# Forget bias and causal mask of a two-layer attention trunk: from bias matmuls and a mask addition to one fused vector operation with the bias read back from DRAM

## The reference

```python
f_logit = (proj[..., 4 * WIDTH:] + b_f_bias[j]).astype(jnp.float32)
log_f = jax.nn.log_sigmoid(f_logit).transpose(0, 2, 1)
...
c = jnp.cumsum(log_f, axis=-1)
...
sc = (jnp.einsum('bhqd,bhkd->bhqk', qb, k, preferred_element_type=jnp.float32) * scale
      + (cq[..., :, None] - c[..., None, :]))
sc = jnp.where(kpos[None, :] <= tq[:, None], sc, -jnp.inf)
p = jax.nn.softmax(sc, axis=-1)
```

## Time and profile before

| | us |
|---|---|
| median of 3 runs | 577.65 (577.51 to 578.0) |
| profiled execution, its time | 577.4 |
| its span | 575.6 |
| TensorE busy | 559.3 |
| VectorE / ScalarE / GpSimd busy | 346.8 / 249.4 / 266.7 |

### The profile page before, as it was taken

How to read it: one execution, slowest core, us unless ns; L and a number is a source line. 1 busy time by engine, 2 the same in 40 slices (tenths; PEclk the granted TensorE clock), 3 DMA queues, 4 the chain that set the end, 5 groups by cost and what they waited for, 6 DMA issues and landing times.

```text
span 575.6 us, 9794 instructions
## 1 busy us (share of the span) xinstructions
PE 559.3 (97%) x3131; PEld 518.3 (90%) x3131; DVE 346.8 (60%) x825; ACT 249.4 (43%) x760; POOL 266.7 (46%) x318
## 2 busy tenths in 40 slices
PE   5699999999999999999999999999999999999998
PEld 4589999999999999988888999999999999998887
DVE  4935859585867677674462674747474747473621
ACT  5534535444453535432454653535353544442400
POOL 5555636354545545333646472727272726260700
PEclk9989999999999999999999999999999999999999
DMA  9532404141313222213432242515140526040221
GB/s 286 164 91 64 139 19 129 29 119 40 106 53 92 65 81 73 73 37 107 110 88 73 75 108 39 108 40 118 28 120 25 116 30 136 16 131 9 73 92 55
DMA packets 77066, 48.34 MB, mean 84 GB/s; under 512 B 3952, under 2 KB 71280, under 8 KB 77040
## 3 DMA queue, kind: packets, MB, share of 16 engines
q1 hardware_dynamic: 77040, 48.02, 30.8%
HBM read 45.91 MB, written 2.10 MB: 83 GB/s over the span
## 4 chain that ended last, share of the span: by engine, by line
PE 94%; DVE 2%; SPq 1%; DMA 1%; ACT 1%; issue 0%; POOL 0%
PE banks L298 25%; PE banks L299 25%; PE banks L300 25%; PE banks L405 5%; PE banks L390 3%; PE banks L357 2%; PE banks L375 2%; PE banks L379 2%; PE banks L374 2%; DMA first_raw<-in_a_w_in_dram 1%; PE banks L378 1%; PE banks L318 1%; SPq L233 1%; DVE sin_t L701 1%; SPq L250 0%; DVE hT_lo L681 0%
## 5 line engine op out<-in xcount | busy, mean ns | idle before, releaser
L964 POOL TENSOR_TENSOR w_lo<-w_raw,w_hi 128x512 fp32r<-128x512 f32 x152 | 193.6, 1300 | 69.9 <-ACT w_hi L517 69.9
L298 PE MATMUL banks<-w_hi,hT_hi 128*128 128x384 f32 x512 | 176.4, 344 | 8.2 <-DVE qkn L736 6.4
L300 PE MATMUL banks<-w_hi,hT_lo 128*128 128x384 f32 x512 | 172.2, 336 | 0.0
L299 PE MATMUL banks<-w_lo,hT_hi 128*128 128x384 f32 x512 | 172.2, 336 | 0.0
L298 PEld LDWEIGHTS banks<-w_hi,hT_hi 128*128 128x128 f32 x512 | 96.8, 189 | 10.0 <-DVE qkn L736 7.0
L979 POOL TENSOR_TENSOR msq<-ssq,eps 128x2 f32<-128x2 f32 x64 | 13.7, 215 | 188.2 <-ACT junk L544 188.2
L517 ACT ACTIVATE w_hi<-w_raw 128x512 fp32r<-128x512 f32 x152 | 87.5, 646 | 24.6 <-DMA w_raw<-in_b_w_in_dram 14.4
L299 PEld LDWEIGHTS banks<-w_lo,hT_hi 128*128 128x128 f32 x512 | 96.9, 189 | 0.1
L300 PEld LDWEIGHTS banks<-w_hi,hT_lo 128*128 128x128 f32 x512 | 96.7, 189 | 0.0
L544 ACT ACTIVATE junk<-banks 128x128 bf16<-128x128 f32 x128 | 34.1, 273 | 117.2 <-PE banks L300 117.2
L814 DVE RECIPROCAL gz<-gz 128x128 f32<-128x128 f32 x64 | 58.1, 930 | 0.5
(11 more groups left out here) (104 smaller groups left out, 877.5 us busy)
## 6 DMA issues: line engine op xcount, KB each, us to landing
w_raw<-in_b_w_in_dram SPq DMA_DIRECT2D x64, 256.0 KB, 3.6
w_raw<-in_a_w_in_dram SPq DMA_DIRECT2D x56, 256.0 KB, 2.9
w_raw<-in_w_out_dram SPq DMA_DIRECT2D x32, 256.0 KB, 3.0
xs<-in_x_dram SPq DMA_DIRECT2D x4, 512.0 KB, 6.6
first_raw<-in_a_w_in_dram SPq DMA_DIRECT2D x8, 256.0 KB, 5.8
out_dram<-xs SPq DMA_DIRECT2D x7, 256.0 KB, 2.5
gz<-in_norm_g_dram SPq DMA_DIRECT2D x2, 512.0 KB, 4.2
cos_t<-in_rope_cos_dram SPq DMA_DIRECT2D x1, 256.0 KB, 5.6
```

The lines of the kernel that those rows point to most:

```text
L298: pe.matmul(dst, ah, bh, start=first and m == 0, stop=False)
L299: pe.matmul(dst, ah, bl, start=False, stop=False)
L300: mm = pe.matmul(dst, al, bh, start=False, stop=last and m == n - 1)
L964: pool.tensor_tensor(w_lo[:, slot, k, :], raw, f32(w_hi[:, slot, k, :]), ALU.subtract).then_inc(wlo_set, by)
```

## The change

The four bias matmuls per head, `crows`, `pick`, `onehot` and the separate mask additions go. Instead:

- VectorE's `maxima` makes one fused operation per tile: it adds a row operand in SBUF to the scores in the bank, multiplies by −1, writes the result to `probs` in SBUF and keeps its minimum, which is the negated row maximum. In layer 0 the operand is `strip` (zeros, and the mask in its last 128 columns), in layer 1 `bias_of[t]`. A one-element memset of `gate` stands ahead of three of the four and takes the wait for the scores.
- ScalarE's `exps` reads `probs` (not the banks), with scale −1, and writes it in place; it waits for each tile's maximum by itself.
- After the scan SP writes c (8 x 512) to a DRAM tensor `c_rows` and, when that has landed, reads the head's row back spread over 128 partitions, once per tile at the tile's width (four transfers, 640 KB, per head). They go where layer 0's rotary tables were. For head 0 this stands ahead of head 2's weight chunks; for head h (1 to 7) it stands after chunk 4 of the job h+1, and waits for the maxima of head h−1, since there is one buffer.
- GpSimd adds the mask to the diagonal block of each of the four (`mask_bias`): for head 0 at the end of `first`, for head h+1 in period h after chunk 4 and before `rstd_qk` of tile 2.
- `f_all` moves to the buffer `rot`, `f_exp` to `sin_t`.

```diff
@@ sync: load_job, load_bias
-            def load_job(layer, h, src_of):
+            def load_job(layer, h, src_of, bias=False):
...
                     load_chunk(w_raw[:, k % RAW, :], src_of(k), raw_in[k % RAW])
+                    if bias and k == RAW:
+                        load_bias(h - 1)
...
+            def load_bias(h):
+
+                wait(sp, max_set, TILES * (HEADS + h) if not isinstance(h, int) or h else 0)
+                for t in T_ORDER:
+                    row = c_rows[bass.ds(h, 1), 0:P * (t + 1)].rearrange("o n -> (o n)")
+                    sp.dma_start(bias_of[t], row.partition_broadcast(P)).then_inc(bias_in, 16)
+
             for layer in range(LAYERS):
-                with sp.Fori(0 if layer else 2, HEADS) as h:
-                    load_job(layer, h, head_src(layer, h))
+                if layer == 1:
+                    for h in range(2):
+                        load_job(layer, h, head_src(layer, h))
+                    sp.wait_ge(f_step, 4)
+                    sp.dma_start(c_rows, f_all).then_inc(c_stored, 16)
+                    sp.wait_ge(c_stored, 16)
+                    load_bias(0)
+                with sp.Fori(2, HEADS) as h:
+                    load_job(layer, h, head_src(layer, h), bias=layer == 1)
                 for c in range(OUT_CHUNKS):
-                    load_job(layer, HEADS + c, out_src(layer, c))
+                    load_job(layer, HEADS + c, out_src(layer, c), bias=layer == 1 and c == 0)
@@ tensor: scores
-                if layer == 1:
-                    pe.wait_ge(c_set, 1)
-                    pe.wait_ge(pick_set, h + 1)
...
-                    if layer == 1:
-
-                        pe.matmul(dst, pick[:, s, :], crows[:, 0:w], start=False, stop=False)
@@ scalar: exps
-                wait(act, p_turned, 3 * g)
...
-                    act.wait_ge(max_set, TILES * g + (n + 1 if n < 2 else TILES))
-                    act.activation(probs[:, P_COL[t]:P_COL[t] + w], banks[:, bank, col:col + w], ACT.Exp,
-                                   bias=negmax[:, t:t + 1], accum_out=rowsum[:, t:t + 1]).then_inc(exp_set, 1)
+                    part = probs[:, P_COL[t]:P_COL[t] + P * (t + 1)]
+                    act.wait_ge(max_set, TILES * g + n + 1)
+                    act.activation(part, part, ACT.Exp, bias=negmax[:, t:t + 1], scale=-1.0,
+                                   accum_out=rowsum[:, t:t + 1]).then_inc(exp_set, 1)
@@ vector: maxima
-                wait(dve, exp_set, TILES * g)
-                mask_tile(0)
+                wait(dve, exp_set, TILES * g)
+                wait(dve, p_turned, 3 * g)
+                if layer == 1:
+                    dve.wait_ge(bias_set, h + 1)
                 for n, t in enumerate(T_ORDER):
                     bank, col = S_AT[t]
-                    if n + 1 < TILES:
-                        mask_tile(n + 1)
-                    dve.wait_ge(mask_added, TILES * g + n + 1)
-                    dve.tensor_reduce(negmax[:, t:t + 1], banks[:, bank, col:col + P * (t + 1)], AX.X, ALU.max,
-                                      negate=True).then_inc(max_set, 1)
+                    w = P * (t + 1)
+                    if n < 3:
+                        dve.wait_ge(s_done, 3 * g + n + 1)
+                        dve.memset(gate[0:1, n:n + 1], 0.0)
+                    dve.tensor_tensor_reduce(out=probs[:, P_COL[t]:P_COL[t] + w], in0=banks[:, bank, col:col + w],
+                                             in1=bias_of[t] if layer else strip[:, SEQ - w:], scale=-1.0,
+                                             scalar=NO_MIN, op0=ALU.add, op1=ALU.min,
+                                             accum_out=negmax[:, t:t + 1]).then_inc(max_set, 1)
@@ gpsimd: mask_bias, at the end of first (layer 1) and in period
+                if layer == 1:
+                    mask_bias(0)
+
+            def mask_bias(h):
+
+                pool.wait_ge(bias_in, 16 * TILES * (h + 1))
+                for t in T_ORDER:
+                    diag = bias_of[t][:, P * t:P * (t + 1)]
+                    added = pool.tensor_tensor(diag, diag, strip[:, SEQ - P:], ALU.add)
+                added.then_inc(bias_set, 1)
...
                 split_w(layer, h + 2, s, (4,))
+                if layer == 1:
+                    mask_bias(h + 1)
                 rstd_qk(layer, h + 1, 2)
```

More of the change, by code:

```diff
@@ L27 @@
 MASKED = -3.0e38
+NO_MIN = 3.0e38
 LO_ROW = 32
@@ L83, in build_trunk @@
         sin_t = sb("sin_t", [P, TILES, 2, P])
-        crows = sb("crows", [P, SEQ], F32R)
-        pick = sb("pick", [P, 2, P], F32R)
         ident = sb("ident", [P, P])
-        mask = sb("mask", [P, P])
+        strip = sb("strip", [P, SEQ])
         junk = sb("junk", [P, 2, P], BF16)
-        onehot = sb("onehot", [P, HEADS])
         wf = sb("wf", [P, KC, LO_ROW + HEADS], F32R)
@@ L101, in build_trunk @@
         rinv = sb("rinv", [P, TILES])
+        gate = sb("gate", [1, TILES])
         banks = ctx.enter_context(nc.psum_tensor("banks", [P, 8, SEQ], F32))
@@ L191, in build_trunk @@
                       (QT_BANK, t, slice(cols.start + CH // 2, cols.stop))]
[L193 to L196, removed]
+        sin_flat = sin_t[:, :, :, :].rearrange("p a b n -> p (a b n)")
+        cos_flat = cos_t[:, :, :, :].rearrange("p a b n -> p (a b n)")
+        f_lo, f_exp, ones = sin_flat[0:HEADS, 0:SEQ], sin_flat[0:HEADS, SEQ:], cos_flat[0:HEADS, SEQ:]
+        f_all = rot[:, :, :, :].rearrange("p a b n -> p (a b n)")[0:HEADS, :]
+        bias_of = {3: sin_flat[:, 0:4 * P], 2: sin_flat[:, 4 * P:7 * P], 1: cos_flat[:, 2 * P:4 * P], 0: sin_flat[:, 7 * P:]}
+        c_rows = nc.dram_tensor("c_rows", (HEADS, SEQ), F32, kind="Internal").ap()
         def normed(layer, t):
@@ L622, in first @@
                 split_w(layer, 1, 1, (6, 7))
-                if layer == 1:
-                    act.wait_ge(f_step, 4)
-                    act.wait_ge(consts_set, 1)
-                    act.activation(crows[0:HEADS, :], f_all, ACT.Copy).then_inc(chi_set, 1)
                 exp_z(layer, 0)
@@ L747, in maxima @@
                 g = HEADS * layer + h
-                def mask_tile(n):
-                    t = T_ORDER[n]
-                    bank, col = S_AT[t]
-                    block_at = banks[:, bank, col + P * t:col + P * (t + 1)]
-                    dve.wait_ge(s_done, 3 * g + min(n, 2) + 1)
-                    dve.tensor_tensor(block_at, block_at, mask[:, :], ALU.add).then_inc(mask_added, 1)
+                if isinstance(g, int) and g == 0:
+                    dve.wait_ge(consts_set, 1)
                 wait(dve, exp_set, TILES * g)
-                mask_tile(0)
+                wait(dve, p_turned, 3 * g)
+                if layer == 1:
+                    dve.wait_ge(bias_set, h + 1)
                 for n, t in enumerate(T_ORDER):
                     bank, col = S_AT[t]
-                    if n + 1 < TILES:
-                        mask_tile(n + 1)
-                    dve.wait_ge(mask_added, TILES * g + n + 1)
-                    dve.tensor_reduce(negmax[:, t:t + 1], banks[:, bank, col:col + P * (t + 1)], AX.X, ALU.max,
-                                      negate=True).then_inc(max_set, 1)
+                    w = P * (t + 1)
[6 more added lines that the diff above has]
+                                             accum_out=negmax[:, t:t + 1]).then_inc(max_set, 1)
             def normalise(layer, h):
@@ L925, in period @@
                 low_y(layer, h)
-                if layer == 1:
-                    set_pick(h + 1, 1 - s)
                 split_qk(layer, h + 1)
@@ L984, in _ @@
             pool.memset(ident[:, :], 0.0)
-            pool.memset(mask[:, :], 0.0)
-            pool.memset(onehot[:, :], 0.0)
-            pool.memset(f32(crows[:, :]), 0.0)
+            pool.memset(strip[:, :], 0.0)
             pool.memset(f32(wf[:, :, :]), 0.0)
```

29 lines of the change are left out of this document (5 added, 24 removed).

## The result

The kernel after takes 581.11 us (580.61 to 581.37, 5 runs) against 577.65 (577.51 to 578.12): ratio 1.0057, interval 1.0042 to 1.0072. It is slower by 0.6%, where I had forecast 575.3 and so a gain of 0.4%. The profiled execution took 580.61 with a span of 578.8, 3.2 us above the span of before (575.6).

A forecast was written before the change was run, and what follows sets the result against it. TensorE was taken to bound the kernel (busy 559.3 of 575.6 us). 577.4 − 4.96 (matmuls) + 2.6 (layer 1's start) = 575.04, with the median 0.25 higher 575.3 us; range 573.0 to 580.5.

The forecast's parts named there:

- The matmuls, 4.96 us: Layer 1: dropping four bias matmuls a head takes 0.62 us off TensorE's chain in each of eight heads, 4.96 us.
- The fused operation, hidden: Mask and maximum of a head on VectorE: taken as 2.6 us, even 4.1 just hidden from TensorE, cost nothing.
- The start, 2.6 us: Layer 1's start: bias through DRAM delays head 2's weight chunks and so the exponentials; TensorE waits once, 2.6 us.
- the burst of the earlier trace: Layer boundary before: 640 KB in three broadcasts, 4.65 us from first issue to landing, used to price the bias loads.
- the chunks' wait: Layer 1's start: 2.6 us of TensorE waiting through late weight chunks, with GpSimd's queue costing 0.8 inside it.
- The later heads, "Cost taken: nothing": Layer 1's later heads: bias loads ahead of chunks 5 to 7 and GpSimd's masks fit the spare, cost nothing.
- The broadcast takes about 2.75 us: Later heads: the share of the spare used by bias loads, 4.65 less 1.9 us for a small transfer's landing.
- spare of 4.8: Later heads: last chunk's split, rstd and norm done by about 402.8, TensorE turning q and k at 407.6.
- every later head waits: Rival: seven later heads wait half a microsecond to 1 us each for chunks or GpSimd, 579 to 582; chance 0.12.

The follow-up runs named there:

- one late load: Changed kernel with one bias load per head, issued behind the last weight chunk, masks at the end of GpSimd's period: 573.4 us, 0.9933; with rstd first 572.85 us, 0.9928.
- both moves together: Changed kernel with later heads' bias loads behind the last weight chunk and GpSimd's mask additions at the end of its period: 575.52 us, 0.9965.

## Why the prediction was wrong

- *The matmuls, 4.96 us.* Right: 0.62 us a head, shown by the 27.94 us of the undisturbed heads and by the kernel without bias.
- *The fused operation, hidden.* Right, and shorter than taken (1.74 for 2.6 us). That it costs nothing is shown by the kernel that has it alone.
- *The start, 2.6 us.* The mechanism was right and the size was short: 3.46. The broadcast was priced at 4.65 us from the burst of the earlier trace rows, and took 8.0. That burst has one load of 4 KB rows and two of 512 bytes, from three tensors; this one has four loads of one row. GpSimd's queue, which I had put inside the chunks' wait at 0.8, cost 1.99 of idle by itself, ahead of the 0.98 at the probabilities. I had followed head 1's late rstd to the maxima only, and not to the norm of tile 0, for which TensorE waits before `qkv` of tile 2. With one late load, putting rstd first took 1.2 off period 1 (29.49 to 28.28). That the chunks still ended where forecast is luck: the first was taken up at 332.50, 1.1 late, and from 331 to 333 the DMA engines moved 313 to 346 GB/s where I had taken 201. (322.85 + 1.9 is 324.75, and the sum goes on from 324.85: a slip of 0.1.)
- *The later heads, "Cost taken: nothing".* This is the step that failed. "The broadcast takes about 2.75 us" of a spare of 4.8; the last chunk's copy moved from 399.40 to 408.67, 9.3 us. The spare of 4.8 was not at fault (2.75 and 1.7 of masks fit into it); the price was, and it wasn't a matter of bytes, by which I had chosen the burst to price from. I should have kept the 4.65 to the kind of load that it was measured on, and put both ends of an unknown price against the spare: at 4.65 + 1.9 it was already gone. The rival "every later head waits" named it at 0.12; it came unevenly: TensorE waited in two heads of seven (3.19 and 0.60 us), and the clock added to the head behind the longer wait. So the rival's 579 to 582 was met, but not by the wait of half a microsecond to 1 us in each head that it spoke of.
- What is shown: both queues' order makes a cost of the slow loads (both moves together take 5.6 us off). What the loads cost depends on three things, each shown by runs: that they are four (512 rows in all) and not one (128 rows), loads and rows not separated, that they read one row 128 times, and which DRAM addresses the stored rows have. What stays open is why the stored rows 2 KB apart are worse than the same 4 or 64 KB apart: a larger tensor may also start elsewhere in DRAM, no run separates pitch from place, and starts 256 or 512 bytes apart in other tensors cost at most 1.0 us in the later heads. Of the two later heads that were hit, the third period is the one whose weights came late before too; why the sixth was the other isn't settled.

## What to carry to other kernels

Price a transfer from one of the same kind, with the same number of loads and rows and the same way of reading, and not by its bytes alone; then put the high end of the price against the spare of every queue that it stands in. Where a broadcast of a small row is needed per head, issue one load. If it must be several, give them a place behind the loads that others wait for, and move their consumer with them: either move without the other made nothing better, and one made the kernel 3.8% slower than before. With one load the place no longer mattered to the time (0.9932 and 0.9933). Before two kernels are compared by a period, compare TensorE's idle time and its granted clock in it: the clock alone made 1.0 and 1.5 us of difference here. A matmul's worth is read from the period between two like instructions, not from its own duration.

## Of the hardware, not expected

- In each of eight heads four loads of 128 rows of 512 bytes (256 KB) in place of one load of 128 rows of 2 KB cost the kernel 7.6 us by the ratios (1.0064 and 0.9932; times 581.49 and 573.23).
- One row read by 128 partitions landed after 3.9 to 6.7 us (medians), 128 rows of the same tensor after 2.9 to 3.5.
- The same stored rows 2, 4 or 64 KB apart gave ratios of 1.0057, 0.9996 and 0.9974; the step from 2 to 4 KB took 5.4 us out of the later heads, and from 4 to 64 the profiles differ mainly by the clock in period 1 (1.5 us). The Trainium skill (DMA: Bandwidth & Descriptors, Latency and other measured facts) has rates that fall at very large row pitches; of these three it was the smallest that was slow, and whether by pitch or by address isn't shown.
- After 1.87 us without work the granted clock averaged 0.57 from 336 to 340 in one kernel (rows 4 KB apart); after 1.99 us in the changed kernel it stayed at 1.00. After waits of 2.71 and 3.19 us it averaged 0.58 and 0.62 over four us. One execution each: the length of a wait alone did not decide.
